# A seventh place for expert weights, and sixteen expert pairs written out instead of looped

## What is computed

```
x = x + concat(z_a, z_b) @ W_out          # this sum is called x1 in the kernel
h2 = RMSNorm(x1)
grp = argmax of 4 coarse logits; top-2 of the 8 experts of that group
out = sum over 32 experts e of combine[:, e] * ((silu(h2 @ w_gate[e]) * (h2 @ w_up[e])) @ w_down[e])
y   = RMSNorm(x1 + out) * g_final
```

## Time and profile before

| | |
|---|---|
| median of 3 runs | 565.57 us (564.02 to 568.11) |
| the profiled execution | 564.8 us |
| its span (first to last instruction) | 563.0 us |
| TensorE matmul busy | 489.6 us (87%) |
| VectorE, ScalarE, GpSimd busy | 247.8, 108.5, 187.2 us |
| mean granted TensorE clock | 0.959 of full speed |
| DMA, mean over the span | 252 GB/s, 141.69 MB |

### The profile page before, as it was taken

The page is one execution under the profiler, slowest core; times in us unless marked ns, Lnnn a source line. Parts: engine busy times, 40 slices in busy tenths (PEclk is TensorE's granted clock), DMA queues, the critical chain, the costliest instruction groups (busy, mean ns, idle before and its releaser), DMA issues.

```text
span 563.0 us, 9101 instructions
## 1 busy us (share of the span) xinstructions
PE 489.6 (87%) x3407; PEld 294.1 (52%) x3408; DVE 247.8 (44%) x478; ACT 108.5 (19%) x230; POOL 187.2 (33%) x282
## 2 busy tenths in 40 slices
PE   6999999999999999996489889898878687388972
PEld 4887777777776455453244444444434343244430
DVE  4139999999945223368222212222121212022236
ACT  5130111111125211121122112121111112012214
POOL 2014728836768001110423333332313313033100
PEclk9999999999999999996799999999989989699988
DMA  8993016000003991029678999999999999998076
GB/s 331 333 399 57 0 57 243 2 0 1 1 1 118 376 415 42 37 87 401 220 293 286 366 383 403 397 398 391 396 384 382 391 394 390 396 402 353 30 284 227
DMA packets 35504, 141.69 MB, mean 252 GB/s; under 512 B 10194, under 2 KB 10210, under 8 KB 23193
## 3 DMA queue, kind: packets, MB, share of 16 engines
q1 hardware_dynamic: 29194, 127.91, 59.8%
q0 software_dynamic: 4960, 9.45, 5.2%
q10 hardware_dynamic: 1327, 4.01, 1.8%
HBM read 134.99 MB, written 13.17 MB: 263 GB/s over the span
## 4 chain that ended last, share of the span: by engine, by line
PE 69%; DMA 15%; DVE 4%; SPq 4%; issue 4%; ACT 3%; ACTq 0%; POOL 0%; POOLq 0%; DVEq 0%
PE bank L1218 25%; PE bank L1301 9%; PE bank L1412 9%; PE bank L1432 8%; PE bank L1407 7%; DMA region_x<-in_w_up 6%; DMA region_w<-in_w_up 5%; SPq L383 4%; PE bank L1211 3%; DMA out<-sb_rows 2%; PE bank L1398 2%; PE bank L1362 1%; PE bank L1422 1%; PE bank L1327 1%; DVE ua L1109 1%
## 5 line engine op out<-in xcount | busy, mean ns | idle before, releaser
L1218 PE MATMUL bank<-region_h,region_w 128*128 128x256 f32 (+1 forms) x576 | 140.6, 406 | 0.0
L1218 PEld LDWEIGHTS bank<-region_h,region_w 128*128 128x128 f32 x576 | 109.2, 190 | 29.8
L1109 DVE TENSOR_TENSOR ua<-ua,bank 128x128 f32<-128x128 f32 x30 | 8.6, 286 | 191.0 <-ACT ua L616 191.0
L1412 PE MATMUL bank<-region_w,z 128*32 128x256 f32 x512 | 47.1, 419 | 14.6 <-DMA region_w<-in_w_up 12.3
L1301 PE MATMUL bank<-region_w,z 128*128 128x512 f32 x128 | 56.7, 596 | 0.2 <-ACT z L559 0.2
L1432 PE MATMUL bank<-region_w,ua 128*32 128x512 f32 x344 | 51.9, 598 | 0.0
L772 POOL COPY gcol<-gidx 64x1 uint32 (+1 forms) x30 | 5.3, 178 | 135.3 <-DVE sb_rows L1104 135.3
L894 DVE SCALAR_TENSOR_TENSOR z<-ub,par,z 128x512 f32<-128x512 f32 x60 | 47.5, 791 | 0.0
L894 DVE SCALAR_TENSOR_TENSOR region_x<-ub,par,region_x 128x512 f32<-128x512 f32 x56 | 46.5, 831 | 0.0
L703 POOL TENSOR_TENSOR ub<-region_x 128x512 f32<-128x512 f32 x4 | 25.3, 6320 | 57.8 <-ACT ub L513 31.1
L1301 PEld LDWEIGHTS bank<-region_w,z 128*128 128x128 f32 x128 | 23.8, 190 | 28.0 <-issue 26.3
(11 more groups left out here) (231 smaller groups left out, 628.3 us busy)
## 6 DMA issues: line engine op xcount, KB each, us to landing
region_w<-in_w_down SPq DMA_DIRECT2D x21, 1024.0 KB, 18.2
region_w<-in_w_gate SPq DMA_DIRECT2D x16, 1024.0 KB, 15.1
region_w<-in_w_up SPq DMA_DIRECT2D x16, 1024.0 KB, 17.1
region_w<-in_w_in SPq DMA_DIRECT2D x4, 2048.0 KB, 18.6
slot<-in_w_gate SPq DMA_DIRECT2D x6, 1024.0 KB, 14.8
slot<-in_w_up SPq DMA_DIRECT2D x6, 1024.0 KB, 14.4
slot<-in_w_down SPq DMA_DIRECT2D x6, 1024.0 KB, 14.8
region_x<-in_w_up SPq DMA_DIRECT2D x5, 1024.0 KB, 26.7
```

Of the source, the lines that this page charges most:

```text
L1218: ins = mm(ps[2 * bank + j][:, 0:LEN[j]], sec[name][:, k, c * P:(c + 1) * P], hT[:, k, CUT[j]], start=(k == 0), stop=(k == KC - 1))
L1412: ins = mm(ps[1][r0:r0 + H, 0:2 * P].rearrange("p (w f) -> p w f", w=2), xT[:, k, half * H:(half + 1) * H], wgu[i][:, :, k, h, :], start=( ...
```

## The change

It does four things.

1. A seventh place. Expert 6 is loaded in advance too: gate and up into region_h over tiles 0 to 3 of x1, the down weights in three pieces into the rest of region_h, pst and a new tile pst2. For this x1 is stored to a new memory tensor x1_rows (tiles 0 to 3 as soon as each is formed, tile 4 behind the loads of expert 3) and comes back into region_h behind the last expert's weights; it is waited for (s_x1r) in the final stage. The seventh place is used once: expert 7 goes to place 0 when expert 0 is done, expert 8 to place 1, and so on, expert 12 to place 5; expert 13 goes to place 0 when expert 7 is done, and from there on each expert waits for the one six before it, as before.
2. The final gain (gfin) gets a place of its own width in hist_b, and the diagonal matrices are made behind VectorE's blocks, not ahead of them, since pst holds weights.
3. The sixteen pairs are written out on TensorE, and the loads of SyncE too, with addresses known when it is built.
4. TensorE reads the two block numbers of the next pair (bounds) inside the shared block of this pair, between the token transposes and the wait for the transposed hidden; the first two are read ahead of the first tokens.

```
+        def slot_of(e):
+            return e if e <= NSLOT else (e - NSLOT - 1) % NSLOT
+        def turn_of(e):
+            return 0 if e <= NSLOT else (e - NSLOT - 1) // NSLOT + 1
+        def before_in_slot(e):
+            return e - NSLOT - 1 if turn_of(e) == 1 else e - NSLOT
-        slot_gu = [reg[:, lo:lo + 2 * PART] for reg, lo, _, _ in places]
+        slot_gu = [reg[:, lo:lo + 2 * PART] for reg, lo, _, _ in places] + [RH[:, 0:2 * PART]]
...
+            def store_x1(t):
+                sp.wait_ge(s_x1, 2 * t + 2)
+                sp.dma_start(x1_dram[t * P:t * P + TROWS[t], :], x1[0:TROWS[t], t, :]).then_inc(s_x1d, 16)
+            for t in range(NT - 1):
+                store_x1(t)
             sp.wait_ge(s_o, NT)
             load_expert(3, 3)
+            store_x1(NT - 1)
             sp.wait_ge(s_h2, NT)
             load_part(4, 0, 4)
...
+            sp.wait_ge(s_x1d, 16 * NT)
+            sp.wait_ge(s_x1t, 2 * NT)
+            for part in range(2):
+                load_part(NSLOT, part, NSLOT)
+            sp.wait_ge(s_hout, 16 * 5)
+            down = parts[2][:, NSLOT, :]
+            for lo, hi, dst in ((0, D, RH[:, 2 * PART:2 * PART + D]), (D, D + DA, pst[:, :]), (D + DA, 2 * D, pst2[:, :])):
+                sp.dma_start(dst, down[:, lo:hi]).then_inc(s_wexp[NSLOT][2], 16)
             for i in range(2):
                 sp.wait_ge(s_h2d[i], 16 * ((NT + 1 - i) // 2))
             sp.wait_ge(s_gath[0], 16)
             load_part(5, 0, 5)
             sp.wait_ge(s_tab, 1)
-            with sp.Fori(1, NE // NSLOT) as it:
-                for i in range(NSLOT):
-                    reload(it, i)
+            for e in range(NSLOT + 1, NE):
+                had = before_in_slot(e)
+                last = sp.value_load(bound[0:1, had + 1:had + 2], min_val=1, max_val=NBLK)
+                sp.wait_ge(s_gu, last)
+                load_part(slot_of(e), 0, e)
+                load_part(slot_of(e), 1, e)
+                sp.wait_ge(s_down, last)
+                load_part(slot_of(e), 2, e)
+            for t in range(NT):
+                sp.dma_start(x1[0:TROWS[t], t, :], x1_dram[t * P:t * P + TROWS[t], :]).then_inc(s_x1r, 16)
...
+            def bounds(m):
+                return [pe.value_load(bound[0:1, 2 * m + j:2 * m + j + 1], min_val=1, max_val=NBLK) for j in (1, 2)]
...
                 tr(ps[2][:, 0:P], hid, ident[:, :]).then_inc(s_hT_ps, 1)
                 tokens(KC // 2, KC).then_inc(s_xt_ps, 1)
+                ahead = meanwhile() if meanwhile else None
                 pe.wait_ge(s_hidT, g + 1)
...
             keep_busy(18)
             pe.wait_ge(s_tab, 1)
+            mine = bounds(0)
             pe.wait_ge(s_mv, 1)
...
-            def pair(it, i):
-                first = pe.value_load(bound[0:1, bass.ds(e, 1)], min_val=0, max_val=NBLK - 1)
-                after = pe.value_load(bound[0:1, bass.ds(e + 1, 1)], min_val=1, max_val=NBLK)
-                end = pe.value_load(bound[0:1, bass.ds(e + 2, 1)], min_val=1, max_val=NBLK)
+            def pair(m, first, after, end):
...
+            for m in range(NPAIR):
+                after, end = mine
+                mine = pair(m, first, after, end)
+                first = end
+            pe.wait_ge(s_x1r, 16 * NT)
```

More of the change, by code:

```diff
@@ L249, in build_step @@
         s_mv = sem("s_mv")
-        s_wexp = [[sem(f"s_wexp{i}_{n}") for n in ("gate", "up", "down")] for i in range(NSLOT)]
+        s_x1d, s_x1r = sem("s_x1d"), sem("s_x1r")
+        s_wexp = [[sem(f"s_wexp{i}_{n}") for n in ("gate", "up", "down")] for i in range(NSLOT + 1)]
         s_yg = [[sem(f"s_yg{k}_{t}") for t in range(NT)] for k in range(2)]
@@ L382, in load_part @@
                 dst = slot_dn[i] if part == 2 else slot_gu[i][:, part * PART:(part + 1) * PART]
-                sp.dma_start(dst, parts[part][:, bass.ds(e, 1), :].rearrange("p e n -> p (e n)"))\
-                  .then_inc(s_wexp[i][part], 16)
+                sp.dma_start(dst, parts[part][:, e, :]).then_inc(s_wexp[i][part], 16)
             def load_expert(i, e):
@@ L1125, in _ @@
                 block_of(pairs, 0)
+            for i, t in enumerate(BY_PE):
+                for k in range(2):
+                    nc.vector.tensor_scalar(diag[i][k], ident[:, :], w12[:, k * NT + t:k * NT + t + 1], None,
+                                            ALU.mult).then_inc(s_diag, 1)
             dve.wait_ge(s_gfin, 16)
+            dve.wait_ge(s_x1r, 16 * NT)
             def add_rows(t, done):
@@ L1399, in tokens, with block_of @@
                 return ins
-            def block_of(g, halves, turn):
+            def bounds(m):
+                return [pe.value_load(bound[0:1, 2 * m + j:2 * m + j + 1], min_val=1, max_val=NBLK) for j in (1, 2)]
+            def block_of(g, experts, meanwhile=None):
+                halves = [slot_of(e) for e in experts]
                 pe.wait_ge(s_xt, g + 1)
@@ L1456, in pair @@
+                ahead = block_of(after - 1, (e, e + 1), (lambda: bounds(m + 1)) if m + 1 < NPAIR else None)
                 with pe.If(end > after):
                     with pe.Fori(after, end) as g:
-                        block_of(g, (i + 1, i + 1), it)
-            with pe.Fori(0, NE // NSLOT) as it:
-                for i in range(0, NSLOT, 2):
-                    pair(it, i)
-            for i in range(0, NE % NSLOT, 2):
-                pair(NE // NSLOT, i)
+                        block_of(g, (e + 1, e + 1))
@@ L1467, in _ @@
+                return ahead
+            first = 0
+            for m in range(NPAIR):
[3 more added lines that the diff above has]
+            pe.wait_ge(s_x1r, 16 * NT)
             pe.wait_ge(s_diag, 2 * len(BY_PE))
```

45 lines of the change are left out of this document (18 added, 27 removed).

## The result

The changed kernel takes **575.11 us** (median of 4, 572.03 to 578.53) against 566.84 us before (median of 4): ratio 1.0126, interval 1.0087 to 1.0164, 7 to 8 us slower. In a second set it was 579.06 against 567.83 us: 1.0193 (1.0148 to 1.0237). The forecast was 563.5 us, in a range up to 569.0.

What follows compares the result with a forecast made beforehand. From some 345 us the DMA engines' rate for weights sets the end, TensorE close behind. The seventh place (1.0 us) plus expert 7 done earlier (1.1 us) give 2.1 us, median 565.57 to 563.5 us, range 558.5 to 569.0.

Steps and rivals of the forecast that it cites:

- Term A: Seventh place: expert 12's 8.7 us lead mostly becomes a queue hole before expert 13; 1.0 us gained, bounds 0 to 3.1.
- Term B: When expert 7 is done: TensorE's gains and losses until then move the end one to one; 1.1 us gained.
- the start: Up to the first product: 2.2 us from early readings against a first move some 2.2 us later; net 0.
- borders: Between pairs up to expert 7: three gaps of issue time close without the block-number readings; 4.27 us less.
- readings: Block numbers read inside the four shared blocks up to expert 7: 0.8 us open in each, 3.2 us more.
- code loading: Rival, chance 0.10: four jumps up to expert 7 wait 2.4 us each for TensorE's code, 9.6 us; 573.1 us.
- later borders and readings don't count: Behind expert 7: borders and readings cost or gain nothing, since the weights come last there.
- Readings hidden: Rival, chance 0.12: block numbers are read while the transposes run, so the 3.2 us don't appear; 560.3 us.
- Expert 6 in the way: Rival, chance 0.13: state and gathers wait for expert 6's gate and up; first move 5.3 us later; 566.6 us.
- The lead kept: Rival, chance 0.08: the hole is filled or the stream runs faster, so the whole 8.7 us arrives; 555.8 us.
- What costs nothing: x1's stores and return (6 us each, in idle DMA time), the diagonals (0.9 us), later borders and readings: no cost.

Runs made afterwards that it cites:

- e15: Changed kernel with TensorE's 30 blocks written out for these inputs, without readings, tests or loops; 566.25 us, ratio 0.9976.
- e13: Kernel before (six places) with TensorE's 30 blocks written out for these inputs, without readings, tests or loops; 568.08 us, ratio 1.0012.
- e14: e9 with TensorE's 30 blocks written out for these inputs, without readings, tests or loops; 562.45 us, ratio 0.9892.
- e9: Changed kernel with its seven places used in turn and expert 6's loads behind expert 5's gate and the state's way out; 568.53 us, ratio 1.0020.
- e1: Kernel before with the sixteen pairs written out and nothing else, six places; 571.63 us, ratio 1.0099.
- e2: e1 with two block numbers read inside the shared block and the first pair's read ahead of the first tokens; 571.98 us, ratio 1.0071.
- e6: Kernel before with the first pair out of the loop, its numbers read early, diagonals made late, six places; 565.95 us, ratio 0.9977.
- e5: Kernel before with x1 stored to memory and brought back behind the last weights, six places; 567.02 us, ratio 1.0001.
- e11: Kernel before with a loop of two rounds of six pairs, then four pairs written out, six places; 575.12 us, ratio 1.0134.
- e10: e9 with the pairs in a loop of two rounds of seven, first and last pair outside; 574.31 us, ratio 1.0147.

## Why the prediction was wrong

**Term A, the hole: right in its mechanism.** The place used once turns the lead into a hole, and what is left was put at 1.0 us. Without code in the way it is e15 against e13, 1.8 us (566.25 against 568.08); the intervals of the two overlap, so this agrees with 1.0 and with next to nothing. And with seven places in turn there is no hole and the lead is 5.6 us (e14 against e13).

**Term B, "all that TensorE gains or loses up to there moves the end one to one": right as a rule, wrong in sum.** From before to after the gate of expert 13 moved by +8.8 us, not -1.1. The account, from the two chains:

- mixer stage and router, +4.4: the state's way out starts at 263.50, not 259.08 us. Nearly all of it is there by the gate of expert 3 (254.09 against 250.00), and it is no effect that I can pin to the change: the ten profiles with seven places have 250.04 (e9) to 254.09, the seven with six places 249.80 (e1) to 252.79 (e13). The middle values are about 1 us apart, so a small part may belong to the change; that isn't shown.
- the start, +1.1 (predicted 0): the way out took 16.34 us, not 12.63, so 3.7 more, 2.8 without the 0.87 of the diagonals, where I had 2.2; from its end to the first product it is 3.05 us, not 5.62, so 2.6 less.
- borders, -4.27 (predicted -4.27): no issue time stands between the early pairs.
- readings, +3.39 (predicted +3.2): 0.81, 0.84, 0.80 and 0.94 us.
- stalls for code, +2.95 (predicted 0): 1.00 and 1.95 us.
- first block at a lower clock, +0.76 (6.54 against 5.78 us). 0.4 us are left over.

**The step that failed is the one that set code loading aside.** I gave it 0.10, "against it: the first round of the loop had the same single jumps over fresh code, with borders of 1.18 to 1.80 us that the readings explain alone". That was read at the jumps, and from the first three pairs. Most of the stalls don't stand there: e1 has none in its first three pairs either, its first is at 334 us; the changed kernel has one in them, of 1.00 us; and three of the four marked above cut a product in two some way behind a jump. The longest, 4.39 us, is at a branch, as the rival had it, but far behind expert 7. That the rival's 573.1 us was near the 575.1 is luck: it had 9.6 us up to expert 7, where 2.95 stand. The changed kernel against e15, by the ratios 1.0126 and 1.0193 against 0.9976, is 8 to 12 us, for stalls and readings together; no run takes one of them alone out of the changed kernel.

**A second step failed: "later borders and readings don't count, since the weights come last there".** From the gate of expert 13 to 499 us TensorE waited for weights once, 2.90 us, and the chain stays with TensorE's blocks. In it stand five pieces of the third kind, 11.4 us, and nine readings in shared blocks, 7.9 us. Some readings also go with a lower clock; the one at 368.88 us in the chain, and the stretch behind it, in which the 16 products of L1469 took 3.23 us, not 1.92, at a mean granted clock of 0.58:

```profile
368.88 1.20 issue
...
370.00:373.30 3.30, 3.22 (x18) 0.72 (x18) 0.00 (x0) 0.00 (x0) 1.35 (x3) 0.58 1.02 396
```

The rule that the prediction had cited and set aside is in the Trainium skill, Runtime: NRT & Kernel Launch, section on instruction fetch mechanics: a taken branch out of what is loaded stalls for a DMA. The runs agree (13.3 us in six pieces at L1448 with jumps, none without, e15). The same section of the Trainium skill prefers full unrolling for that reason. Here e1 (1.0099) speaks against it, since written-out pairs still have jumps over the blocks that aren't there.

From the packets (20 more for twelve bodies more, e1) I estimate a pair at 27 KB, so a loop of three pairs at 82 KB, which stays, and one of six at 164 KB, which doesn't. The same section of the Trainium skill gives TensorE 128 KiB for instructions, and both runs agree with that.

**A third miss, in what the kernel before is bound by.** Right: the weights set its end (e13). But then closing borders could gain nothing at six places (e2, e6, e13), and could only count because the change itself opens the hole and ties the end to TensorE. At six places TensorE's sequencer had 14.7 us of waits for weights in which lost time could vanish; in the changed kernel, behind the hole and up to the wait for expert 31, it has 2.9.

**Behind expert 13.** The stream took 169.6 us from the gate of expert 13 (360.47) to the landing of expert 31's up part (530.05), against 167.5 before (351.69 to 519.15), where I had 1 us less. The landing before, from the chain:

```profile
490.40 28.75 DMA region_w<-in_w_up
```

Stalls of over 4 us at 414 and 428 us also take the clock: the block behind each runs 5.2 and 6.1 us, not 3.7. In the tail 2.6 us more pass, 1.9 of them in the block at 530.14 us (5.84 us, against 3.92 at 519.24), behind a wait of 4.9 us for its weights.

**Rivals.** Readings hidden: no, 0.8 us each. Expert 6 in the way: in part, the first move came 2.8 us later, not 5.3. The lead kept: only without stalls and with places in turn, and then 5.6 of 8.7. Code loading: yes, though not where it was put. **What costs nothing** held for x1's round trip (e5, 1.0001; no wait for s_x1r on the chain), and not for the later borders and readings.

## What to carry to other kernels

A place for weights that is used once moves a wait, it doesn't remove one: follow the queue place by place, then ask who has to be done for the next free place, since from there that engine's every delay is on the path. Before writing a loop out, or making its body longer, look at the instruction queue behind the first round: if it brings nothing, the loop costs no code behind that round, while written-out code with jumps, or a body that no longer stays, can be paid at a branch or in the middle of a product. A version with the same places and no jumps tells the places from the code in one run, as long as one remembers what else went with the jumps (here the readings).

## What the runs showed of the hardware

- A loop body of three pairs (82 KB of code, estimated from the count of packets) runs from 330 to 519 us without one instruction packet; one of six or seven pairs is brought again in its second round, with 7.66 us of issue time at the jump back in e11 and 12.14 us in e10.
- A packet of code takes 1.1 us in the queue and arrives in time beside full weight loads if the code is in a row: 27 packets and no stall (e13 to e15). At or behind jumps TensorE stood still for 1 to 4.4 us at some of the packets.
- Behind the stalls of over 4 us the granted clock was at half. Stretches of the changed kernel at 418.5 and 433 us:

```profile
418.50:421.50 3.00, 2.51 (x24) 1.32 (x28) 0.00 (x0) 0.00 (x0) 0.00 (x0) 0.50 1.03 287
433.00:438.00 5.00, 5.00 (x49) 2.72 (x52) 0.00 (x0) 0.00 (x0) 0.00 (x0) 0.50 1.02 388
```

- The mixer stage, the same products in all runs, ended anywhere from 249.8 to 254.1 us (gate of expert 3), with or without a stretch at half clock in the first 40 us. A difference of 4 us in one profile is not yet an effect; the medians are.

What stays open: why one packet behind a jump costs nothing or 1 us at one place and 4.4 us at another, how the 8 to 12 us part into stalls and readings, and the 0.4 us of the account. A general kernel with seven places and no jumps wasn't found; e14 is right for these inputs alone, and of the general ones e6 (0.9977, 0.9946 to 1.0008) is the fastest, not measurably faster than the kernel before.
